# Delta rule decay exponents: from bf16 row products on TensorE to f32 sums on GpSimd and VectorE

## The reference, cut to what matters

```
gc    = cumsum(g)                      # log decay, per chunk
decay = exp(where(incl, gc[:, None] - gc[None, :], -inf))
a_mat = where(strict, (kb @ k.T) * decay, 0)        # kb = k * beta
sol   = solve_triangular(a_mat + I, rhs)
qk    = (q @ k.T) * decay
# scan over the chunks:
v_new = u - w @ s ;  o = q_dec @ s + qk @ v_new ;  s = s * d + k_dec.T @ v_new
```

## Time and profile before

| | us |
|---|---|
| median of 3 runs | 3360.06 |
| range of the runs | 3359.83 to 3364.39 |
| span of the profiled execution | 3362.7 |
| TensorE busy | 3184.5 (95%) |
| TensorE weight loads busy | 2066.8 (61%) |
| VectorE busy | 1745.8 (52%) |
| ScalarE busy | 1475.9 (44%) |
| GpSimd busy | 637.6 (19%) |
| first L961 (level 0) of layer 0 and of layer 3 | 229.49, 2312.00 |

### The profile page before, as it was taken

How to read it: one execution, slowest core, us unless ns; L and a number is a source line. 1 busy time by engine, 2 the same in 40 slices (tenths; PEclk the granted TensorE clock), 3 DMA queues, 4 the chain that set the end, 5 groups by cost and what they waited for, 6 DMA issues and landing times. The chain is left out here.

```text
span 3362.7 us, 57300 instructions
## 1 busy us (share of the span) xinstructions
PE 3184.5 (95%) x22569; PEld 2066.8 (61%) x22569; DVE 1745.8 (52%) x3567; ACT 1475.9 (44%) x3027; POOL 637.6 (19%) x524
## 2 busy tenths in 40 slices
PE   5779999999999999999999999897999999999998
PEld 2347777777777764455445555444676767767663
DVE  1146666666666652244433334244666766666642
ACT  3135545545545531156423445234455555555521
POOL 0013322322232220011001010002323232232300
PEclk9789999999999999999999999897999999999999
DMA  9811111111111127022311012001112111111135
GB/s 376 305 40 39 41 45 34 50 41 45 50 41 45 31 65 261 0 61 67 123 32 38 25 39 88 32 16 50 36 43 55 42 54 38 54 40 42 42 109 193
DMA packets 216679, 238.16 MB, mean 71 GB/s; under 512 B 19290, under 2 KB 159780, under 8 KB 216292
## 3 DMA queue, kind: packets, MB, share of 16 engines
q1 hardware_dynamic: 216420, 234.57, 21.7%
HBM read 214.87 MB, written 19.66 MB: 70 GB/s over the span
## 5 line engine op out<-in xcount | busy, mean ns | idle before, releaser
L917 PE MATMUL ps<-hT,W 128*128 128x512 f32 (+1 forms) x2656 | 1007.9, 507 | 2.9 <-DVEq L192 2.0
L917 PEld LDWEIGHTS ps<-hT,W 128*128 128x128 f32 x2656 | 467.6, 192 | 206.0 <-issue 164.9
L1349 DVE CAST_PREDICATED arena<-mask,ps 128x384 bf16<-128x384 uint32 x448 | 252.5, 564 | 242.1 <-PE ps L986 180.0
L1168 ACT CAST arena<-ps 128x384 bf16<-128x384 f32 x384 | 166.5, 479 | 339.4 <-PE ps L973 339.0
L2352 PE MATMUL ps<-arena 128*128 128x512 f32 x712 | 311.1, 595 | 2.7 <-SPq L192 2.5
L1351 DVE CAST_PREDICATED arena<-mask,ps 128x384 bf16<-128x384 uint32 x448 | 249.9, 558 | 0.0
L2352 PEld LDWEIGHTS ps<-arena 128*128 128x128 f32 x712 | 134.6, 191 | 167.4 <-issue 162.6
L1987 PE MATMUL ps<-hT,W 128*128 128x512 f32 (+1 forms) x608 | 218.2, 493 | 0.9 <-DMA W<-in_att_w_in 0.7
L1461 POOL TENSOR_TENSOR arena<-arena 128x768 f32<-128x768 f32 (+1 forms) x32 | 43.5, 1360 | 921.2 <-ACT arena L1204 921.2
L1324 DVE SCALAR_TENSOR_TENSOR arena<-arena,vec 128x770 f32<-128x770 f32 (+1 forms) x192 | 189.6, 988 | 6.8
L986 PEld LDWEIGHTS ps<-arena 128*128 128x128 bf16 x2304 | 147.1, 99 | 50.8 <-issue 45.7
(11 more groups left out here) (290 smaller groups left out, 6105.9 us busy)
## 6 DMA issues: line engine op xcount, KB each, us to landing
arena<-in_ada_w SPq DMA_DIRECT2D x24, 2048.0 KB, 19.7
W<-in_gdn_w_in SPq DMA_DIRECT2D x95, 512.0 KB, 4.0
W<-decay_rows SPq DMA_DIRECT2D x64, 384.0 KB, 4.9
arena<-in_gdn_w_out SPq DMA_DIRECT2D x32, 512.0 KB, 10.3
W<-in_gdn_w_out SPq DMA_DIRECT2D x30, 512.0 KB, 3.4
arena<-gated SPq DMA_DIRECT2D x32, 384.0 KB, 8.2
gated<-arena SPq DMA_DIRECT2D x24, 384.0 KB, 2.4
W<-in_att_w_in SPq DMA_DIRECT2D x16, 512.0 KB, 4.0
```

Of the source, the lines that this page charges most:

```text
L917: mm = pe.matmul(ps[:, b, 0:t1 - t0], w[:, i, :], env.hT[:, i, t0:t1], start=(i == 0), stop=(i == KD - 1))
L1168: act.copy(half_cols(Xb[d], s, d), ps[:, 2 * d, 0:384].rearrange("p (c b s) -> p c b s", c=NT, s=s)).then_inc(*inxe.up(m, lv, d))
L1349: dve.copy_predicated(half_cols(Mb[d], s, d), wide(env.m4[:, d, lv]), src_m).then_inc(*inm.up(m, lv, d, "m"))
```

## The change

Per unit and direction the row gc, sent as bf16 parts before, is now stored once in f32 (`decay_sums`), broadcast to 128 partitions by a transfer into `gexp`, gets the cap added on GpSimd and the per-partition column (log beta - gc, kept in the table as COL) on VectorE; ScalarE takes the exponential of it from SBUF for both halves at once. GpSimd's and VectorE's sums of unit m + 1 stand in slot n of unit m: on GpSimd after the splits of NAT, on VectorE at position 8 ahead of the level's copies. For unit 0 they stand ahead of slot -2. The buffer `gexp` is single: the next load waits for the exponential. The E sets leave the plan, `FILL` starts with 6, 5 instead of 10, 8, and the head of the layer loses the split into parts and its stores. Some semaphores are shared under common names.

```diff
+G_AT = 8
-FILL = (10, 8, 4, 5, 5, 4, 5, 5, 3, 5, 5, 4, 5, 5, 5, 4, 7, 0)
+FILL = (6, 5, 4, 5, 5, 4, 5, 5, 3, 5, 5, 4, 5, 5, 5, 4, 7, 0)
-        if unit:
-            beside = order.pop(0) if tile else wide.pop(0)
-            front = FRONT_OF_E[int(beside[1])]
-            add(beside, bank, 0, front)
-            for i in range(4):
-                add(f"E{i}", i)
-            add(beside, bank, front)
-            bank = 13 - bank
...
-        def load_el(m):
+        def load_g(m):
             for d in BOTH:
-                sp.dma_start(v.ELb[32 * d:32 * d + 3], a["split"][d, m, 0:3]).then_inc(*el.up(m, 3 * d))
-                sp.dma_start(v.ELb[32 * d + 6:32 * d + 9], a["split"][d, m, 3:6]).then_inc(*el.up(m, 3 * d + 1))
-                sp.dma_start(v.ERb[32 * d + 3:32 * d + 6], a["split"][d, m, 0:3]).then_inc(*el.up(m, 3 * d + 2))
+                sp.dma_start(v.gexp[:, d], a["sums"][d, m].partition_broadcast(P)).then_inc(*gl.up(m, d))
...
-                sp.wait_ge(ad.sem, ad.at(n, "E3"))
-                load_el(m + 1)
+                sp.wait_ge(gexp.sem, gexp.at(m, 1))
+                load_g(m + 1)
...
-            if use[0] == "E":
-                d, half = part // 2, part % 2
-                if i == 0:
-                    pe.wait_ge(el.sem, el.at(m, 5))
-                    pe.wait_ge(mtf.sem, mtf.at(m - 1, d))
-                    mm = pe.matmul(ps[:, b, 0:384], env.identb[:], v.capb[:, d].unsqueeze(1).broadcast_to([P, 3, P]),
-                                   start=True, stop=True, skip_group_check=True)
-                else:
-                    c = 3 * half + i - 1
-                    mm = pe.matmul(ps[:, b, cols(i - 1)], v.ELb[32 * d:32 * d + 9, cols(c)], v.ERb[32 * d:32 * d + 9, cols(c)],
-                                   start=False, stop=True, skip_group_check=True)
...
+        def decay(m):
+            for d in BOTH:
+                act.wait_ge(garg.sem, garg.at(m, d))
+                act.wait_ge(ro.sem, ro.at(m - 2, NT - 1, d))
+                act.activation(flat(QKD[m % 2][d]), v.gexp[:, d], ACT.Exp).then_inc(*gexp.up(m, d))
...
+                if p == 0 and m in U:
+                    decay(m)
...
-        dve.tensor_copy(parts[0], R2).then_inc(*t_dve.up("hi"))
...
-        dve.tensor_copy(parts[2], R4).then_inc(*t_dve.up("low"))
...
-                    dve.wait_ge(aev.sem, aev.at(m - 1, ("E1", "E3")[d]))
+                    dve.wait_ge(gexp.sem, gexp.at(m, d))
...
+        def exponents(m):
+            for d in BOTH:
+                dve.wait_ge(gcap.sem, gcap.at(m, d))
+                g = v.gexp[:, d].rearrange("p (c n) -> p c n", c=NT)
+                dve.tensor_tensor(g, g, tab[:, COL, :, d, m:m + 1].broadcast_to([P, NT, P]), ALU.add).then_inc(*garg.up(m, d))
...
+        exponents(0)
         for n in SLOTS:
             m = n + 1
             for p in range(POS):
+                if p == G_AT and m in U and m + 1 in U:
+                    exponents(m + 1)
                 if m in U and (p in (1, 17) or (p >= 2 and p % 2 == 0)):
                     levels(m, p)
...
+        def capped(m):
+            for d in BOTH:
+                pool.wait_ge(gl.sem, gl.at(m, 1))
+                g = v.gexp[:, d].rearrange("p (c n) -> p c n", c=NT)
+                cap = (env.cap_f, env.cap_b)[d].unsqueeze(1).broadcast_to([P, NT, P])
+                pool.tensor_tensor(g, g, cap, ALU.add).then_inc(*gcap.up(m, d))
+
+        capped(0)
...
+            if m in U and m + 1 in U:
+                capped(m + 1)
```

More of the change, by code:

```diff
@@ L564, in add @@
                 before[n, use] = (b, last_in.get(b))
-                if use[0] != "E":
-                    last_in[b] = (n, use)
+                last_in[b] = (n, use)
             first = max(CT, lo) if use == "G0" and short else lo
@@ L639, in gdn_phase @@
     w_in = a["gdn_w_in"][j]
-    NEG, KDEC, DCH = range(3)
+    NEG, KDEC, DCH, COL = range(4)
     v = carve(env, [("pad", (2, PADW)), ("acc", (2, CONVW)), ("q", (T,)), ("k", (T,)), ("kS", (T,)), ("sq", (T,)),
@@ L661, in gdn_phase @@
     t_ld = seq("t_ld", [(k,) for k in ("dt0", "dt1", "al0", "al1")], 16)
-    t_set = seq("t_set", [(k,) for k in ("sgn", "neg", "zero", "wpad", "r1", "r0f", "r0b", "pad", "xb0", "xb1", "el", "er", "erm0", "erm1", "off", "nid",
-                                         "capf", "capb", "hot0", "hot1")])
+    t_set = seq("t_set", [(k,) for k in ("sgn", "neg", "zero", "wpad", "r1", "r0f", "r0b", "pad", "xb0", "xb1", "off", "nid", "hot0", "hot1")])
     t_pad = seq("t_pad", [("w",)])
     t_mm = seq("t_mm", [(k,) for k in ("rows", "turn", "total")])
-    t_dve = seq("t_dve", [(k,) for k in ("z0", "z1", "abs", "pos", "sp", "g", "gcf", "gcb", "lnb", "hi", "r1", "mid", "r2", "low", "tok0", "tok1",
+    t_dve = seq("t_dve", [(k,) for k in ("z0", "z1", "abs", "pos", "sp", "g", "gcf", "gcb", "lnb", "tok0", "tok1",
                                          "kd0", "kd1", "kt0", "kt1", "neg")])
     t_act = seq("t_act", [(k,) for k in ("al", "e1", "l1", "eg", "neg0", "neg1", "kdec", "dch0", "dch1")])
-    t_row = seq("t_row", [(d, k) for d in BOTH for k in range(7)], 16)
+    t_row = seq("t_row", [(d, k) for d in BOTH for k in range(2)], 16)
     wx = seq("w_x", [(n,) for n in TILES], 16)
@@ L673, in gdn_phase @@
     wz = seq("w_z", [(m,) for m in U], 16)
-    el = seq("el", [(m, i) for m in U for i in range(6)], 16)
+    gl = seq("g_row", [(m, d) for m in U for d in BOTH], 16)
+    gcap = seq("g_capped", [(m, d) for m in U for d in BOTH])
+    garg = seq("g_arg", [(m, d) for m in U for d in BOTH])
+    gexp = seq("g_exp", [(m, d) for m in U for d in BOTH])
     eg = seq("eg", [(m, d) for m in U for d in BOTH], 16)
@@ L759, in padcols @@
         return slice(o, o + P)
-    tab = v.table.rearrange("p (k c d) n -> p k c d n", k=3, c=NT)
-    R0, R1, R2, R3, R4, R5 = (flat(t) for t in (MF[0], MF[1], MT[0], MT[1], NAT[0], NAT[1]))
+    tab = v.table.rearrange("p (k c d) n -> p k c d n", k=4, c=NT)
+    R0, R1, R2, R3, R5 = (flat(t) for t in (MF[0], MF[1], MT[0], MT[1], NAT[1]))
     tokT = QKD[0][0]
-    parts = [flat(QKD[1][i // 2])[:, 384 * (i % 2):384 * (i % 2) + 384].bitcast(BF16) for i in range(3)]
     hot = QKD[0][1]
@@ L825, in sync @@
             sp.dma_start(alc[32 * d:32 * d + 16], column("gdn_a_log", d)).then_inc(*t_ld.up(f"al{d}"))
-        sp.wait_ge(t_dve.sem, t_dve.at("low"))
+        sp.wait_ge(t_dve.sem, t_dve.at("gcb"))
         sp.wait_ge(t_act.sem, t_act.at("eg"))
         for d in BOTH:
[L829 to L835, removed]
+            sp.dma_start(a["sums"][d], R2[32 * d:32 * d + 16]).then_inc(*t_row.up(d, 0))
+            sp.dma_start(a["rows"][d], R5[32 * d:32 * d + 16]).then_inc(*t_row.up(d, 1))
+        sp.wait_ge(t_row.sem, t_row.at(1, 1))
+        load_g(0)
         for n in SLOTS:
@@ L1121, in keep @@
             act.wait_ge(ad.sem, ad.at(n, use))
[L1122 to L1126, removed]
+            if use[0] == "X":
                 act.wait_ge(convx.sem, convx.at(n - 1, 3))
@@ L1506, in lru_phase @@
     lama = Sig(env, "lru_lam_act", 1)
-    wu = seq("w_u", per(*one), 16)
-    wz = seq("w_z", per(*one), 16)
+    wu = Seq(env, "gdn_w_x", per(*one), 16)
+    wz = Seq(env, "gdn_w_z", per(*one), 16)
     wg = seq("w_g", per(*four), 16)
-    st = seq("st", per(*one), 16)
+    st = Seq(env, "gdn_st", per(*one), 16)
     ud = seq("u_done", per(*one))
@@ L1519, in lru_phase @@
     sq = seq("root", per(*two))
-    cv = seq("conv", per(*four))
+    cv = Seq(env, "gdn_convv", per(*four))
     iu = seq("iu", per(*[(d, i) for d in range(2) for i in range(2)]))
@@ L1523, in lru_phase @@
     scn = seq("scan", per((0,), (1,), (2,)))
-    og = seq("og", per(*two))
+    og = Seq(env, "gdn_og", per(*two))
     U0 = D
@@ L1846, in att_phase @@
     cst = seq("cst", [(k,) for k in ("band", "dup0", "dup1", "pdup0", "pdup1")])
-    wkv = seq("w_kv", [(g, i) for g in G for i in range(2)], 16)
-    wq = seq("w_q", [(g, u) for g in G for u in range(2)], 16)
+    wkv = Seq(env, "gdn_w_v", [(g, i) for g in G for i in range(2)], 16)
+    wq = Seq(env, "gdn_w_x", [(g, u) for g in G for u in range(2)], 16)
     wz = [seq("w_z", [(g,) for g in G], 16), Seq(env, "gdn_w_z", [(g,) for g in G], 16)]
-    st = seq("st", [(g,) for g in G], 16)
-    ad = seq("fill_done", order)
-    aev = seq("fill_act", [key for key in order if key[1] not in on_dve])
+    st = Seq(env, "gdn_st", [(g,) for g in G], 16)
+    ad = Seq(env, "gdn_fill_done", order)
+    aev = Seq(env, "gdn_fill_kept", [key for key in order if key[1] not in on_dve])
     dev = seq("fill_dve", [key for key in order if key[1] in on_dve])
@@ L1855, in att_phase @@
     rad = seq("rope", [(g, k) for g in G for k in ("k", 0, 1)])
-    szd = seq("silu_z", [(g,) for g in G])
+    szd = Seq(env, "lru_silu_z", [(g,) for g in G])
     sc = seq("scores", [(p, i) for p in PAIRS for i in range(2)])
@@ L2518 @@
     aps["rows"] = nc.dram_tensor("decay_rows", (2, 16, T), F32).ap()
```

(2 more changed lines are left out.)

25 lines of the change are left out of this document (5 added, 20 removed).

## The result

The change made the kernel slower by a third of a per cent: 3373.64 us median of 5 runs against 3360.06, ratio 1.0032 with a 95% interval of 1.002 to 1.0045. Forecast were 3341.5 us. The measured time lies just past the upper end of the range, and near the second of the rivals.

The account below looks back on a forecast made before the run. TensorE's in-order list was taken to bound the slots with inversion work. The terms -68.5 + 31.6 + 17.5 + 0.8 = -18.6 us, applied to the median 3360.06, gave 3341.5 us, range 3311 to 3372.

Parts of the forecast that it names:

- the second of the rivals: Even: one full block of 1.45 us in each slot's front, +4.5 us, 3365 us; chance 0.16.
- What leaves TensorE: Four E product sets per unit leave TensorE's list, 2.14 us in each of 32 units: 68.5 us removed.
- The sums at position 8: VectorE's two sums ahead of level 3's copies hold TensorE's products of position 9: 31.6 us added.
- The front: Slot start up to level 0: GpSimd's casts and L1451 delay NAT and score on VectorE, 17.5 us added.
- FILL's moved units "worth nothing": 3.2 units of projection work move to later positions, as long there: worth nothing where TensorE never waits.
- Edits at nothing: GpSimd's sums and the two broadcasts per unit come in time, under cover; together with the layers' ends 0.8 us added.
- The third rival: Slower: GpSimd blocks VectorE's NAT and score at the front of 28 slots, 63 us, 3387 us; chance 0.12.

Follow-up runs that it names:

- the best version: Changed kernel with GpSimd's split of NAT waiting for the score, VectorE's sums at position 12 and FILL starting 8, 6: 3290.33 us, ratio 0.9783 to the kernel before.

## Why the prediction was wrong, point by point

- *What leaves TensorE*, 68.5 us: right. With the new waits removed (the best version) the kernel is 73 us faster, of which 68.3 us lie between the first and the last level 0 of the two layers in the traces. Its slots are shorter by 2.24 and 2.69 us in the first layer and 1.88 and 2.65 in the last (odd n, then even), against the 2.14 taken for each.
- *The sums at position 8*, 31.6 us: right, 27 to 31 in three pairs of runs. In the changed kernel L1336 starts at 690.16 directly behind the convolution, without idle before it. It was right by kind of slot, too. With the sums at 12 instead of 8, both with the split after the score, the slots with even and odd n are 0.58 and 0.95 us shorter in the first layer and 1.61 and 0.93 in the last, where 0.6, 1.1, 1.8 and 0.5 were taken.
- *The front*, 17.5 us: this is the step that failed. The mechanism was named, and the pair's 3.3 us was on the table; the term was too small, because the step gave the score's first user 0.7 to 2 us of cover. That user is the scan's output product (`qkd` in `scan`). Side 1 of it is due at B+7.3, and an unblocked score behind a late NAT is done only at about B+7.1, so there are 0.2 us of cover and the block is paid whole. In the last layer level 0's copies, behind the score in VectorE's queue, pass it on to L949. Measured: 40 us for the score, by the run with the split after it, and 5 to 8 for NAT. By the traces the waits of the score's block are 33 us: 1.44 us per slot in the first layer and 1.43 with odd n in the last, where 0.5 and 1.1 were taken, and 0.75 with even n in the last for 0.4. The other 8 us are the lower granted clock in five slots, for which the prediction has no term.
- *FILL's moved units "worth nothing"*: wrong by 12 us. The prediction adds "where TensorE never waits", and that condition did not hold: moving work moved x0 beside x1 and X1's last product beside o1, and two turns of a PSUM bank became waits.
- *Edits at nothing*: GpSimd's sums (1.8 us each) and the broadcasts (4.2 us to landing) were in time. VectorE's sums waited 4.3 us for GpSimd in the whole span, at the heads of the layers.
- The sum with the measured sizes, from the best version back: -73 + 12 (plan) + 31 (middle) + 40 (score) = +10 us; measured +0.32%, 11 us. The sum is made of differences between whole runs, so the clock's 8 us are inside the 40. The second rival's case (one full block of 1.45 us in each front) comes nearest: it happened in three kinds of slot of four, and its time is 9 us short for want of the plan's 12. That its 40.6 us meet the measured 40 is in part luck: the waits alone are 33, and the clock fills the rest. The third rival's mechanism was at work as well: over the four kinds of slot the score's block is 1.27 us on average, about the 1.3 from which it decides. But with NAT's 5 to 8 us the whole front cost 45 to 48 us, not its 63.

## What to carry to other kernels

When work leaves the bounding engine, list every reader of what the other engines make in that stretch, each with its own turn, from the semaphores and not from the one reader that waits today; the first to run dry decides, and the trace of before does not show it, because it never waited. An overlap of VectorE and GpSimd that costs nothing under cover is the first thing to look for once the cover goes, and it may be bought off by one wait on the engine with slack. And an order that a planner derives from shares should be printed for both kernels: here no line of the change names the product that lost 1.6 us. Last, before a wait is priced by its length, look at the granted clock of each slot: here five slots lost 1.6 to 1.7 us each on top of their waits.

## What the runs showed of the hardware

VectorE's product of two SBUF operands took 2.40 us instead of 0.95 beside a GpSimd instruction that reads SBUF, with GpSimd held in turn (L1435 2.35 for 1.65). Beside a GpSimd instruction that only writes, a memset, it took 0.95 to 0.96.

In the slots of the delta-rule layers, the first of each layer left out, TensorE's granted clock was 1.00 in most and 0.97 in some. In the latter it fell from 2.4 to 1.2 GHz behind a wait of TensorE of 0.8 to 2.0 us, and the slot took 1.6 to 1.7 us longer than one of its kind. That happened in five slots of the changed kernel, in six with the sums at 12, in six with FILL 10, 8, in six with the identities by transfer, in five of the best version with FILL 10, 8, in one of it with the sums at 8, and in none of the kernel before and of the best version. Waits of the same length stand in other slots without it.

TensorE's granted clock also differed between executions in a stretch that no edit touches, the end of attention. Windows of the kernel before (columns as above):

```profile
2110.00:2130.00 20.00, 15.99 (x90) 9.71 (x90) 7.86 (x19) 7.60 (x17) 0.00 (x0) 0.83 0.00 0
2130.00:2150.00 20.00, 14.77 (x70) 7.96 (x70) 3.32 (x11) 5.29 (x12) 0.00 (x0) 0.83 0.00 1
```

and of the changed kernel, in the same work:

```profile
2125.00:2145.00 20.00, 14.04 (x86) 8.36 (x82) 10.12 (x27) 8.90 (x21) 0.00 (x0) 0.91 0.01 2
2145.00:2165.00 20.00, 14.80 (x73) 7.64 (x74) 2.86 (x11) 2.97 (x6) 0.00 (x0) 1.00 0.16 54
```

TensorE is busy only about three quarters of these windows in both, in short pieces between ScalarE's steps; part of the time at 1.2 GHz instead of 2.4, and more of it in the first than in the second. The stretch from 2087 to the projection behind it took 7.4 us longer at the lower clock, more than half of the effect studied here.
